# Seven products of quarters for three pairs of FFN blocks instead of two, with half of the weight sums made by accumulating transfers

## The reference, cut to what matters

```python
def swiglu(u, w_in, w_out):
    gt, up = jnp.split(u @ w_in, 2, axis=-1)     # u: 256 x 1024, w_in: 1024 x 5632
    return (jax.nn.silu(gt) * up) @ w_out        # w_out: 2816 x 1024

# layers 0 and 1 of the first part, and the one layer of the second part:
h = h + swiglu(rmsnorm(h, norm_ffn[layer]), ffn_w_in[layer], ffn_w_out[layer])
x = x + (jax.nn.silu(h2 @ ffn_w1[l]) * (h2 @ ffn_w3[l])) @ ffn_w2[l]
```

## Time and profile before

| | before |
|---|---|
| median of the three runs | 1043.04 us |
| span of the profiled execution, first to last instruction | 1041.3 us |
| TensorE matmul busy | 1033.9 us, 99% |
| VectorE busy | 843.5 us, 81% |
| ScalarE busy | 593.8 us, 57% |
| GpSimd busy | 21.6 us, 2% |
| bytes moved by DMA | 182.97 MB, mean 176 GB/s |
| granted TensorE clock | full in all 40 slices |

### The profile page before, as it was taken

How to read it: one execution, slowest core, us unless ns; L and a number is a source line. 1 busy time by engine, 2 the same in 40 slices (tenths; PEclk the granted TensorE clock), 3 DMA queues, 4 the chain that set the end, 5 groups by cost and what they waited for, 6 DMA issues and landing times.

```text
span 1041.3 us, 13328 instructions
## 1 busy us (share of the span) xinstructions
PE 1033.9 (99%) x4884; PEld 841.5 (81%) x4884; DVE 843.5 (81%) x1366; ACT 593.8 (57%) x897; POOL 21.6 (2%) x30
## 2 busy tenths in 40 slices
PE   9999999999999999999999999999999999999998
PEld 7877778888888888788888888787777888888887
DVE  6877889797868987896887788989978878878684
ACT  6845474655646646655656564638656446466462
POOL 0221000000000000000000000000000000000000
PEclk9999999999999999999999999999999999999999
DMA  8762478382456534683743653544444468739243
GB/s 278 228 206 83 128 249 270 122 277 87 142 187 187 180 134 142 216 283 126 246 140 96 221 169 122 158 151 154 147 160 135 148 189 258 242 122 303 85 153 107
DMA packets 135706, 182.97 MB, mean 176 GB/s; under 512 B 12588, under 2 KB 82730, under 8 KB 135514
## 3 DMA queue, kind: packets, MB, share of 16 engines
q1 hardware_dynamic: 134130, 178.36, 53.2%
q0 software_dynamic: 1104, 3.21, 1.2%
q10 hardware_dynamic: 408, 0.56, 0.2%
HBM read 181.03 MB, written 1.05 MB: 175 GB/s over the span
## 4 chain that ended last, share of the span: by engine, by line
PE 92%; DVE 5%; ACT 2%; issue 1%; DVEq 0%; ACTq 0%
PE ps L2169 13%; PE ps L2174 13%; PE ps L2170 13%; PE ps L2186 7%; PE ps L2187 7%; PE ps L2191 7%; PE ps L2309 4%; PE ps L2311 4%; PE ps L2314 4%; PE ps L2152 3%; PE ps L2154 3%; PE ps L2153 3%; DVE wlo L1175 1%; PE ps L2259 1%; PE ps L2242 1%; PE ps L2733 1%
## 5 line engine op out<-in xcount | busy, mean ns | idle before, releaser
L1175 DVE TENSOR_TENSOR wlo<-raw,whi 128x1024 fp32r<-128x1024 f32 (+1 forms) x290 | 349.4, 1232 | 28.8 <-ACT whi L631 27.1
L631 ACT ACTIVATE whi<-raw 128x1024 fp32r<-128x1024 f32 (+1 forms) x290 | 295.5, 1053 | 106.9 <-DMA raw<-in_ffn_w_in 33.1
L2169 PE MATMUL ps<-whi,ath 128*128 128x512 f32 (+1 forms) x688 | 274.5, 400 | 2.2 <-ACT whi L631 0.7
L2170 PE MATMUL ps<-whi,atl 128*128 128x512 f32 (+1 forms) x688 | 266.4, 388 | 0.0
L2174 PE MATMUL ps<-wlo,ath 128*128 128x512 f32 (+1 forms) x688 | 182.9, 388 | 0.0
L2169 PEld LDWEIGHTS ps<-whi,ath 128*128 128x128 f32 x688 | 129.3, 188 | 35.6 <-issue 5.9
L2174 PEld LDWEIGHTS ps<-wlo,ath 128*128 128x128 f32 x688 | 128.2, 188 | 27.4 <-DVE wlo L1175 0.6
L2170 PEld LDWEIGHTS ps<-whi,atl 128*128 128x128 f32 x688 | 129.4, 188 | 24.7 <-issue 0.5
L2186 PE MATMUL ps<-whi,brh 128*128 128x512 f32 x272 | 106.5, 392 | 0.0
L2187 PE MATMUL ps<-whi,brl 128*128 128x512 f32 x272 | 105.9, 389 | 0.0
L1189 DVE TENSOR_TENSOR wlo<-work,whi 128x1024 fp32r<-128x1024 f32 x84 | 98.7, 1220 | 4.5 <-ACT whi L648 4.5
(11 more groups left out here) (380 smaller groups left out, 1415.4 us busy)
## 6 DMA issues: line engine op xcount, KB each, us to landing
raw<-in_ffn_w_in SPq DMA_DIRECT2D x112, 256.0 KB, 3.5
raw<-in_w_in SPq DMA_DIRECT2D x104, 256.0 KB, 2.9
raw<-in_ffn_w SPq DMA_DIRECT2D x100, 256.0 KB, 3.5
raw<-in_ffn_w_out SPq DMA_DIRECT2D x88, 256.0 KB, 3.5
work<-in_ffn_w_in SPq DMA_DIRECT2D x64, 256.0 KB, 4.8
raw<-in_a_w_in SPq DMA_DIRECT2D x48, 256.0 KB, 4.3
raw<-in_b_w_in SPq DMA_DIRECT2D x48, 256.0 KB, 3.1
work<-in_ffn_w SPq DMA_DIRECT2D x32, 256.0 KB, 4.6
```

Source lines behind the costliest of these rows:

```text
L631: a_(unit_view(whi, slot, w), unit_view(raw, slot, w), ACT.Copy).then_inc(hi_ready, 1)
L1175: v_.tensor_tensor(unit_view(wlo, slot, w), unit_view(raw, slot, w), unit_view(whi, slot, w), ALU.subtract).then_inc(lo_ready, 1)
L2169: mm(ps[bk + apart * t][:, 0:w], ath[:, k, t * P:(t + 1) * P], rh[:, kk, :], start=k == 0, stop=False)
L2170: mm(ps[bk + apart * t][:, 0:w], atl[:, k, t * P:(t + 1) * P], rh[:, kk, :], start=False, stop=False)
```

## The change

`PAIRED` becomes (3, 6, 9): three pairs of blocks, of which the third is the last two blocks, so that it has no block after it. The plan of an FFN grows from 78 to 84 units. SP no longer loads the quarters; a new function on POOL does, and it makes t1 and t3 by itself: it loads one quarter into the buffer and then lets a second transfer add the other quarter to it (`accum_op=ALU.add`). To make sums out of what were differences, signs of the token sums and two of the results (`rneg`) are turned. DVE keeps t2 and t4, four sums for each pair.

```diff
-PAIRED = (4, 8)
+PAIRED = (3, 6, 9)
...
+                if k == 0:
+                    pool.wait_ge(unit_used, u0 + 1)
+                    part("t1", "b11", j)
+                    part("b22", "b22", j)
+                    part("t3", "b12", j)
+                    there("t1", False)
+                    part("t1", "b12", j, accum_op=ALU.add)
+                    there("b22")
+                    part("b11", "b11", j)
+                    there("t3", False)
+                    part("t3", "b22", j, accum_op=ALU.add)
+                    there("b11")
+                    part("b21", "b21", j)
+                else:
+                    free("b11")
+                    part("b11", "b11", j)
+                    free("t3")
+                    part("t3", "b12", j)
+                    free("t1")
+                    part("t1", "b11", j)
+                    there("t3", False)
+                    part("t3", "b22", j, accum_op=ALU.add)
+                    there("t1", False)
+                    part("t1", "b12", j, accum_op=ALU.add)
+                    pool.wait_ge(sem("pair_sums"), sums_done(n, f"{k - 1}_t4_1"))
+                    free("b21")
+                    there("b11")
+                    part("b21", "b21", j)
+                    free("b22")
+                    there("b21")
+                    part("b22", "b22", j)
...
                     feed(b + 19)
                     if more:
-                        weight_sum(k + 1, "t1", 0)
+                        weight_sum(k + 1, "t2", 0)
                     feed(b + 20)
                     if more:
-                        weight_sum(k + 1, "t1", 1)
+                        weight_sum(k + 1, "t2", 1)
                     turn(j + 2 + FB * n)
                     feed(b + 21)
                     if more:
-                        weight_sum(k + 1, "t3", 0)
+                        weight_sum(k + 1, "t4", 0)
...
+                    if j + 2 == FB:
+                        product(b + 14, 1, *a22, onto=True, middle=lambda: hid_turn(hids + 2))
+                        pe.wait_ge(hid_lo, j + 1 + FB * n)
+                        down_unit((b + 16) % RING, 2, False, False, b + 17, brh, brl)
+                        hid_turn(hids + 4)
+                        down_unit((b + 17) % RING, 3, False, False, b + 18, brh, brl)
+                        return
```

More of the change, by code:

```diff
@@ L71, in ffn_plan @@
             plan += half[:6] + [("down", j - 1, k) for k in range(2)] + half[6:]
-            plan += [("up", j + 2, c) for c in range(4)]
-            plan += [("down", j + b, k) for b in range(2) for k in range(2)]
+            if j + 2 < FB:
+                plan += [("up", j + 2, c) for c in range(4)]
+                plan += [("down", j + b, k) for b in range(2) for k in range(2)]
+            else:
+                plan += [("down", j, k) for k in range(2)]
             j += 3
@@ L87, in plan_at @@
     return PLAN.index(unit)
[L91 to L99, removed]
 SUMS = ["a0", "a1", "s1", "s2", "s3", "s4", "l1", "l2", "l3", "l4"]
 for _k in range(len(PAIRED)):
-    SUMS += [f"{_k}_{_t}_{_i}" for _t in ("t1", "t3", "t2", "t4") for _i in range(2)] + [f"{_k}_{_c}" for _c in ("c22", "c11", "c21")]
+    SUMS += [f"{_k}_{_t}_{_i}" for _t in ("t2", "t4") for _i in range(2)] + [f"{_k}_{_c}" for _c in ("c22", "c11", "c21")]
 COPIES = 4 + 3 * len(PAIRED)
@@ L411, in sums_done, with parts_there @@
             return len(SUMS) * n + SUMS.index(name) + 1
[L413 to L418, removed]
+        part_loaded = {b: sem("pair_whole_loaded") for b in ("b11", "b22", "b21")}
+        part_loaded |= {b: sem(f"pair_{b}_loaded") for b in ("t1", "t3")}
+        def parts_there(n, k, name, added=True):
+            done = len(PAIRED) * n + k
+            if name in ("t1", "t3"):
+                return 128 * done + (128 if added else 64)
+            return 64 * (3 * done + (("b11", "b21", "b22") if k else ("b22", "b11", "b21")).index(name) + 1)
         def tap(name, n):
@@ L502, in load_ffn @@
                         load(u, [(v[:, nb, :], down_w[k * P:(k + 1) * P, nb * 512:(nb + 1) * 512]) for nb in range(2)])
[L503 to L508, removed]
-                        for dst, src in up(pair_part(name), 2 * (b[1] == "2") + int(h), block * 256):
-                            nc.sync.dma_start(dst, src).then_inc(part_loaded[b], 16)
             load_in(U_A, D["a_w_in"][0], 0, ahead=load_x)
@@ L2301, in body, with product @@
                             ffn_down(j, c - 4, j + FB * n, u % RING, u + 1, j == 1 and c == 4, False)
-                def product(u, bank, hi, lo, onto=False):
+                def product(u, bank, hi, lo, onto=False, middle=None):
                     for i in range(2):
+                        if i and middle is not None:
+                            middle()
                         pe.wait_ge(hi_ready, u + i + 1)
@@ L2368, in ffn @@
                 pe.wait_ge(hid_lo, FB * (n + 1))
-                end = [(last, 2, False, False), (last + 1, 3, False, True)]
+                end = [(last, 0, False, False), (last + 1, 1, False, True)]
                 if r < 4:
```

121 lines of the change are left out of this document (70 added, 51 removed).

## The result

| | before | after |
|---|---|---|
| median of the runs, us | 1043.1 (1043.0 to 1043.3) | 1210.6 (1207.8 to 1211.8) |
| ratio, 95% interval | | 1.160 (1.159 to 1.162) |
| span of the profiled execution, us | 1041.3 | 1207.9 |
| TensorE without work in the span, us | 7.4 | 148.0 |

The changed kernel is 16% slower. I had said slower, 1101 us, with 1135 as the upper end: the direction was right, and the loss of 168 us was nearly three times the 58 us of the forecast.

The account below looks back on a forecast made before the run. TensorE bounds the kernel, busy 1033.9 of 1041.3 us; late transfers decide. Per FFN 2 x 10.7 - 2.72 + 0.7 = +19.4 us, three FFNs +58: 1043 + 58 = 1101 us; 8-in-10 range 1036 to 1135, the forecast's own 1072 to 1135.

Parts of the forecast that it names:

- Removed matmuls, -8.2 us: TensorE: one more pair in each of three FFNs saves 3 x 12 matmuls of 0.227 us, 8.2 us, all on the path.
- The passages: From one pair to the next, twice per FFN: t2's quarters 10.7 us late, TensorE waiting in the fourth up unit.
- The choice of 1.5: Price of an accumulating transfer in plain ones, from three movements instead of two; bounds once (6.9 us late), twice (13.6).
- The first pair, just in time: Start of each FFN: b21 ready at 40.5 us against a limit of 40.5; at twice the price 2.8 us late.
- I give each half, 187 GB/s: DMA in a passage: GpSimd's and SyncE's queues share 373 GB/s evenly; SyncE's 4.2 MB take 22.5 us, to 234.5.
- Inside a pair the load of VectorE is as before: VectorE: 2.4 us more per FFN, but 24 units and 4 sums in a pair as before; hidden, counted as nothing.
- Rival A: DMA queues: transfers keep up, 1037 us, or 1042 with the bare chain's lateness; chance 0.22 faster, 0.05 gain eaten up.
- could only add: TensorE's clock: what a rest does to it can't be had from the rows; it could only add; no size.
- Tail of the FFN, +0.7 us each: Third pair's end, no block after it: 0.5 us wait for `hid`, 0.2 for `brh` and `brl`; 2.1 us in all.
- B: GpSimd's issues limit, not the bus: 6.4 us late per passage, 1075 us; shares 0.70 with the forecast.
- C: Accumulating transfers: additions much slower than two reads, for example four times, 1229 us; chance 0.03.
- D: VectorE becomes the bound; rejected at about 39 us of work in a pair of 47.7 us; no chance given.

Follow-up runs that it names:

- 6: Changed kernel with t2 and t4 of the second and third pair summed inside that pair instead of behind the pair before: 1130.1 us, 1.084.
- 7: Kernel 6 with the second transfers of t1 and t3 plain (overwriting) instead of adding: 1113.2 us, 1.066.
- 8: Three pairs, all eight sums on VectorE, t1 and t3 included; GpSimd loads four plain quarters per pair, nothing adding: 1067.6 us, 1.024.
- 9: Kernel 8 with each group of quarter loads waiting for a later place in VectorE's order, t3 later, t2 inside the next pair: 1042.0 us, 0.9993.
- kernel 5: Changed kernel with two pairs per FFN, PAIRED = (3, 9), adding transfers kept, second pair's t2 and t4 summed inside that pair: 1104.1 us, 1.059.
- Experiment 11: Changed kernel with 60 matmuls by zero weights where TensorE waits in each of six passages; results as before: 1209.0 us, 1.159.
- experiment 1: Program of transfers alone, without the model, plain and adding, on one queue or both: plain 324 to 350 GB/s, adding 189, adding beside SyncE's plain 235.
- kernel 10: Kernel 6 with the first load of the next pair's quarters waiting until VectorE has split the two down units inside the pair: 1127.6 us, 1.081.
- kernel 2: Changed kernel with the second transfers into t1 and t3 plain, overwriting instead of adding; sums wrong: 1157.6 us, 1.110.
- 12: Kernel 9 with the quarters on SyncE's own queue, half a quarter behind one of SyncE's units, none on GpSimd: 1058.3 us, 1.015.
- 3: Changed kernel without the second transfers of t1 and t3, five quarters per pair instead of seven; sums incomplete: 1082.7 us, 1.038.

## Why the prediction was wrong, point by point

The way from the changed kernel back to the kernel before, in steps that were run:

| from, to | us | what it takes away |
|---|---|---|
| after, 6 | 1210.6 to 1130.1 | -80.5: VectorE's and TensorE's wait for the next pair's quarters |
| 6, 7 | 1130.1 to 1113.2 | -16.9: the extra price of adding |
| 7, 8 | 1113.2 to 1067.6 | -45.6: three of the seven quarters that GpSimd moves for a pair, with its waits for their landings; VectorE makes four sums more |
| 8, 9 | 1067.6 to 1042.0 | -25.6: bursts on the second queue; the sums t3 and t2 stand later too |

- **Removed matmuls, -8.2 us.** Right: 4848 matmuls. Kernel 9 has the 36 matmuls less, but only 5.4 us of the 8.2 in TensorE's busy time (1028.5), and 3.6 us more idle, of which 2.2 us are the tail (below). Why its matmuls take 2.8 us more than the forecast has, I didn't settle.
- **The passages.** The place, the waiting instruction and the releaser were right. The size: 10.7 us was forecast with an addition as 1.5 transfers, 13.6 with 2, and 14.3 was measured. The choice of 1.5 was the first mis-sized term, worth 6 x 2.9 = 17 us. I had bounds of 1 and 2 and went to the middle by counting movements; nothing measured stood behind that, and 1.7 to 1.9 was measured. That 14.3 is so near to 13.6 is luck, for two errors cancel. From the first load of t1 to the sum t2 my sum at twice has 34.1 us (206.6 to 240.7), and the six passages took 37.8 to 39.7. The time until TensorE needed the fourth unit, which I had at 20.5 us, was 23.6 to 25.5 us, for TensorE had waited in between as well (2.7 us for `hid` in the first). In GB/s it looks like this: the 9.45 MB of the passage at 244 to 266 GB/s need 36 to 39 us, and the first one took 39.7.
- **The first pair, just in time.** For its quarters this held: b21 was issued at 164.84, and no sum of the first pair waited for a transfer. But the stretch 158 to 182 us has TensorE busy 16.9 of 24 us, and none of it idle in the kernel before. What it waits for are `hid`, `whi` and `brl`, behind units of SyncE that land late, 7.1, 6.6 and 6.4 us in the three FFNs, 20 us that the sum doesn't have.
- **"I give each half, 187 GB/s. SyncE's 4.2 MB take 22.5 us", and "Inside a pair the load of VectorE is as before ... I count nothing".** This is the step that failed most. I let SyncE's units be late and asked only what their traffic does to the quarters, never what lateness does to them. Rival A even says that some may come late "without harm". They have six slots of ring, but ScalarE rounds in program order, so a unit that lands 4 us late also holds `sil`, `brh` and then `hid`, `brl` and the transposes. Kernel 6, where t2 waits for nothing on the path, is still 87 us over before, and kernel 5 with two roomy pairs 61. Of the changed kernel's 148 us of idle time 86.1 are the passages, 7.4 were there before and 2.2 are the tail; the other 52 are these waits (`whi` 26, `hid` 18, `brl` 8), forecast at 0. So the 110 us between 1101 and 1210.6 are about 52 us of these waits, 34 us of busy time (+26.0 where -8.2 was forecast) and 22 us in the passages (86.1 where 6 x 10.7 = 64 was forecast).
- **The clock, "could only add".** It fell in each passage, to 0.50, as the windows show. Experiment 11 takes the fall away and the time stays, 1209.0 against 1210.6 us. So it added next to nothing. With the clock at 0.99 TensorE's busy time, less six fills of 14.0 us, is still 24.6 us above 4848 matmuls at the old rate. This part of the 34 us by which the busy time missed its forecast is not the fall in the passages; what it is stays open.
- **Tail of the FFN, +0.7 us each.** The size was right and the place wrong. Kernel 9 has almost no other waits, so it shows the term: TensorE waits 0.3 us for `hid` once, and at the end of two of the three FFNs 1.1 us for `x`, which VectorE adds up late. The kernel before has none of these waits. That is 2.5 us where 2.1 was forecast.

```profile
310.04 0.66 PE L2281 MATMUL ps<-con,x 128*128 128x128 f32 x4 [1.12 <-DVE x L1263]
```

- **Rivals.** A was refuted, by a wait of 19.25 us where it needs none. B fell: in the passage the DMA share is above 1, and issues begin every 0.7 to 0.8 us but for one gap; their records grow to 3.1 us only by overlapping. In experiment 1, 16 adding issues do take 19.6 us where plain ones take 11.7, with the share at 1.21, so there they wait on a full queue. C was refuted by experiment 1. Its 1229 us is near the result by accident: it put all of it down to the price of adding, which is worth 17 to 53 us. D fell: VectorE has 86% in kernel 9, and no matmul waits there for `wlo`.

## What to carry to other kernels

When a second DMA queue is filled, price the transfers of the first one again: read their landing time in the profile, and follow what stands behind the engine that consumes them in program order. Two accumulating transfers of 256 KB save one vector operation of 1.2 us, and each costs nearly two plain ones, which both queues pay; here VectorE had the room for the sums and the DMA, in its peaks, had none. Prefetches should be released at a place in the consumer's order where the other queue rests, not as soon as their buffer is free: together with two sums that were moved to suit it, that was worth 25.6 us here with plain transfers, and 2.4 us with additions.

## What the runs showed of the hardware that I had not expected

- Adding transfers fill the DMA engines at 189 GB/s (share 1.21) where plain ones of the same shape do 324 to 350. In rows of 4 KB it is 408 against 210:

```profile
137.00:141.00 4.00, 0.72 (x2) 1.00 1.02 408
152.00:162.00 10.00, 1.40 (x2) 1.00 1.06 210
```

  The Trainium skill ("DMA: Bandwidth & Descriptors", section "Where 436 GB/s comes from") has the fabric's ceiling at 435 GB/s, and says that transfers between HBM and SBUF are bound by the HBM side, at about 358 GB/s. The first figure alone, which the prediction took, is thus not the page's rule for these loads. Neither is quite what the trace has: 408 GB/s with 4 KB rows, and at most 380 in the rows and windows shown of the kernels' rows of 1 and 2 KB.
- The record of an issue on GpSimd, 0.72 us by itself, grows to 3.1 us with additions (4.0 in kernel 10), and stays at 0.72 with as many plain ones (kernel 2). The records overlap, so their length isn't time that the engine is held.
- TensorE's clock was at 0.50 (1.2 GHz) while the engine rested in the passages, and was at 0.92 to 1.00 in the window of 4 us that begins 4 us after work had resumed.
- The median landing of SyncE's 256 KB of `in_ffn_w_out` goes with the loss over these kernels, but loosely: 3.5 us before, 3.7 in kernel 9, 4.5 in 12, 4.9 in 5, 5.5 in 3, 6.4 in 8, 7.5 in 2, 7.7 in 7, 8.9 in 10, 9.0 in 6 and 9.1 in the changed one. Kernel 5 loses more than 8, and 2 more than 6.
